# Multiplying the first two weight chunks behind six norms as a pair, contraction tile by contraction tile

## The reference, cut to what matters

```python
def _rmsnorm(x, w):
    xf = x.astype(jnp.float32)
    y = xf * lax.rsqrt(jnp.mean(xf * xf, axis=-1, keepdims=True) + EPS)
    return (y * w.astype(jnp.float32)).astype(x.dtype)
```

```python
def _conv_ffn(h, w_up, conv_w, w_down):
    u = _causal_dwconv(jnp.matmul(h, w_up), conv_w)
    gate, val = jnp.split(u, 2, axis=-1)
    return jnp.matmul(jax.nn.silu(gate) * val, w_down)
```

```python
        x = ffn_half_step(x, mx[0:3], g_ffn1[l], w_ffn1_gu[l], w_ffn1_down[l])
        hx = modulated_norm(x, g_mix[l], mx[3], mx[4])
        out_x = fourier_sgu_mixer(hx, ...)      # or attention in layer 1
        x = x + mx[5] * out_x
        x = ffn_half_step(x, mx[6:9], g_ffn2[l], w_ffn2_gu[l], w_ffn2_down[l])
```

## Time and profile before

| | before |
|---|---|
| median of 3 runs | 2116.26 us |
| the profiled execution | 2117.21 us |
| its span in the profile | 2115.1 us |
| TensorE busy (matmul) | 2043.2 us, 97% |
| VectorE busy | 1172.4 us, 55% |
| ScalarE busy | 821.3 us, 39% |
| mean granted TensorE clock | 0.992 |

### The profile page before, as it was taken

One profiled execution on the slowest core, in us unless ns is written; L12 is line 12 of the kernel. 1 busy time (PEld: TensorE's weight loads), 2 busy tenths in 40 slices (PEclk: granted clock), 3 DMA queues, 4 the chain that ended last, 5 costly groups with the idle time before them and its releaser, 6 DMA issues.

```text
span 2115.1 us, 30883 instructions
## 1 busy us (share of the span) xinstructions
PE 2043.2 (97%) x13253; PEld 1788.8 (85%) x13254; DVE 1172.4 (55%) x1579; ACT 821.3 (39%) x1049; POOL 224.8 (11%) x185
## 2 busy tenths in 40 slices
PE   6988999999999999999999999999999999999998
PEld 6985997999888888889888888888888888869998
DVE  6767555767653654453555442235766744655454
ACT  5642454655532222243342222234222223455444
POOL 1000000403111001100101001110100111001001
PEclk9999999999999999999999999999999999999999
DMA  6424654454642543352344332234545533304553
GB/s 240 158 84 179 221 199 180 148 182 162 227 161 93 189 146 135 107 187 89 120 159 153 122 136 88 82 127 168 196 162 201 189 116 113 125 20 160 172 182 114
DMA packets 54136, 317.05 MB, mean 150 GB/s; under 512 B 6000, under 2 KB 12400, under 8 KB 23792
## 3 DMA queue, kind: packets, MB, share of 16 engines
q1 hardware_dynamic: 50848, 308.99, 41.1%
q10 hardware_dynamic: 3152, 6.10, 0.8%
HBM read 314.01 MB, written 1.05 MB: 149 GB/s over the span
## 4 chain that ended last, share of the span: by engine, by line
PE 83%; DVE 8%; ACT 5%; issue 3%; DMA 1%; SPq 0%; DVEq 0%; ACTq 0%
PE psum L279 26%; PE psum L280 25%; PE psum L281 25%; ACT w_hi L255 3%; DVE w_lo L263 1%; PE psum L1316 1%; PE psum L1710 1%; DVE work L454 1%; DMA raw<-in_w_in_r 0%; DVE xc L1497 0%; PE psum L1330 0%; DVE small L1377 0%; DVE normed_lo L1890 0%; PE psum L918 0%; DVE work L1023 0%
## 5 line engine op out<-in xcount | busy, mean ns | idle before, releaser
L279 PE MATMUL psum<-normed_hi,w_hi 128*128 128x256 f32 (+1 forms) x2600 | 859.3, 330 | 20.0 <-DVE normed_lo L461 9.0
L280 PE MATMUL psum<-normed_lo,w_hi 128*128 128x256 f32 (+1 forms) x2600 | 848.8, 326 | 0.0
L281 PE MATMUL psum<-normed_hi,w_lo 128*128 128x256 f32 (+1 forms) x2600 | 848.5, 326 | 0.0
L263 DVE TENSOR_TENSOR w_lo<-raw,w_hi 128x2048 fp32r<-128x2048 f32 (+1 forms) x246 | 510.7, 2076 | 401.7 <-ACT w_hi L255 400.9
L279 PEld LDWEIGHTS psum<-normed_hi,w_hi 128*128 128x128 f32 x2600 | 492.9, 190 | 73.7 <-issue 23.6
L280 PEld LDWEIGHTS psum<-normed_lo,w_hi 128*128 128x128 f32 x2600 | 493.3, 190 | 43.0 <-issue 1.2
L281 PEld LDWEIGHTS psum<-normed_hi,w_lo 128*128 128x128 f32 x2600 | 492.9, 190 | 42.3
L255 ACT ACTIVATE w_hi<-raw 128x2048 fp32r<-128x2048 f32 (+1 forms) x246 | 421.7, 1714 | 167.4 <-PE psum L281 157.3
L279 PE MATMUL psum<-h_hi,w_hi 128*128 128x512 f32 (+1 forms) x913 | 310.6, 340 | 2.0 <-POOL h_lo L1655 1.7
L281 PE MATMUL psum<-h_hi,w_lo 128*128 128x512 f32 (+1 forms) x913 | 309.4, 339 | 0.0
L280 PE MATMUL psum<-h_lo,w_hi 128*128 128x512 f32 (+1 forms) x913 | 309.4, 339 | 0.0
(11 more groups left out here) (380 smaller groups left out, 1358.7 us busy)
## 6 DMA issues: line engine op xcount, KB each, us to landing
raw<-in_mod SPq DMA_DIRECT2D x72, 1024.0 KB, 4.7
raw<-in_a_up SPq DMA_DIRECT2D x42, 1024.0 KB, 4.8
raw<-in_b_up SPq DMA_DIRECT2D x42, 1024.0 KB, 4.8
raw<-in_ffn_up SPq DMA_DIRECT2D x22, 1024.0 KB, 4.9
raw<-in_a_down SPq DMA_DIRECT2D x32, 704.0 KB, 4.1
raw<-in_b_down SPq DMA_DIRECT2D x32, 704.0 KB, 4.1
raw<-in_ffn_down SPq DMA_DIRECT2D x16, 704.0 KB, 4.0
raw<-in_wo SPq DMA_DIRECT2D x8, 1024.0 KB, 4.8
```

What stands on the lines that cost most here:

```text
L263: dve.tensor_tensor(w_lo[:, slot, 0:size], raw[:, raw_slot(("main", g)), 0:size], w_hi[:, slot, 0:size].bitcast(F32), ALU.subtract).then_i ...
L279: pe.matmul(out, lh, rh, start=first, stop=False, skip_group_check=group)
L280: pe.matmul(out, lh, rl, start=False, stop=False, skip_group_check=group)
L281: return pe.matmul(out, ll, rh, start=False, stop=last, skip_group_check=group)
```

## The change

A method `pe_pair` takes the place of `pe_first` and of `ready_at_first` ahead of six jobs. `pe_feature_major` first waits for both of the first two chunks (their banks and their low parts), then hands both to `pe_pair`, and goes on with the third chunk as before. For the plain norms the first four contraction tiles are multiplied for both chunks (12 matmuls a tile), then tiles 4 to 7 of chunk 0, then tiles 4 to 7 of chunk 1. For a `HalfNorm` the first half of the columns is done for both chunks tile by tile, then the second half chunk by chunk; the sums of the second half move to the place behind tile 0. For the `FinalNorm` the order is context half of chunk 0, the 48 small matmuls, context half of chunk 1, sequence half of chunk 0, sequence half of chunk 1. `ready_at_first` and `pe_first` of `HalfNorm` stay for other jobs.

```diff
--- before.py
+++ after.py
@@ -280,10 +280,17 @@
             pe.matmul(out, lh, rl, start=False, stop=False, skip_group_check=group)
             return pe.matmul(out, ll, rh, start=False, stop=last, skip_group_check=group)
 
-        def pe_feature_major(pe, job, act_hi, act_lo, span, n_tiles=2, k_tiles=KT, before_k=None, after_chunk=None, k_order=None, in_halves=None):
+        def pe_feature_major(pe, job, act_hi, act_lo, span, n_tiles=2, k_tiles=KT, before_k=None, after_chunk=None, k_order=None, in_halves=None,
+                             first_pair=None):
 
             k_order = k_order or tuple(range(k_tiles))
-            for s in steps(job):
+            if first_pair is not None:
+                pair = steps(job)[:2]
+                for s in pair:
+                    bank_free(pe, s)
+                    pe.wait_ge(lo_ready, s.g + 1)
+                first_pair(pe, pair, act_hi, act_lo)
+            for s in steps(job)[0 if first_pair is None else 2:]:
                 bank_free(pe, s)
                 pe.wait_ge(lo_ready, s.g + 1)
                 if in_halves is not None and s.c in in_halves:
@@ -303,6 +310,14 @@
                 if after_chunk is not None:
                     after_chunk(s.c)
 
+        def pair_tile(pe, s, act_hi, act_lo, k, src, dst):
+
+            for n in range(2):
+                w = slice((n * KT + k) * P, (n * KT + k + 1) * P)
+                mm = three_passes(pe, psum[:, s.bank + n, dst], (w_hi[:, s.slot, w], w_lo[:, s.slot, w]),
+                                  (act_hi[:, k, src], act_lo[:, k, src]), k == 0, k == KT - 1)
+            return mm
+
         def pe_token_major(pe, job, act_hi, act_lo, span, after_tile=None):
 
             for s in steps(job):
@@ -476,6 +491,18 @@
             def ready(self, pe, k):
 
                 pe.wait_ge(n_lo, self.split_base + (k + 1) * self.halves)
+
+            def pe_pair(self, pe, pair, act_hi, act_lo):
+
+                for k in range(KT // 2):
+                    self.ready(pe, k)
+                    for s in pair:
+                        pair_tile(pe, s, act_hi, act_lo, k, self.span, slice(0, self.w))
+                for s in pair:
+                    for k in range(KT // 2, KT):
+                        self.ready(pe, k)
+                        mm = pair_tile(pe, s, act_hi, act_lo, k, self.span, slice(0, self.w))
+                    mm.then_inc(chunk_done, 1)
 
             def ready_at_first(self, pe):
 
@@ -1534,9 +1561,9 @@
                     if half:
                         pe_feature_major(pe, up, self.norm.hi, self.norm.lo, slice(0, self.w))
                     elif self.w > T:
-                        pe_feature_major(pe, up, xn_hi, xn_lo, slice(0, self.w), in_halves={0: self.norm.pe_first})
+                        pe_feature_major(pe, up, xn_hi, xn_lo, slice(0, self.w), first_pair=self.norm.pe_pair)
                     else:
-                        pe_feature_major(pe, up, self.norm.hi, self.norm.lo, slice(0, self.w), before_k=self.norm.ready_at_first(pe))
+                        pe_feature_major(pe, up, self.norm.hi, self.norm.lo, slice(0, self.w), first_pair=self.norm.pe_pair)
 
                     if half and late is not None:
                         late()
@@ -1822,6 +1849,22 @@
                                               (act_hi[:, k, t], act_lo[:, k, t]), k == 0, k == k_tiles - 1)
                 return mm
 
+            def pe_pair(self, pe, pair, act_hi, act_lo):
+
+                t = slice(0, T)
+                for k in range(KT):
+                    if k == 1:
+                        self.pe_sums(pe, 1)
+                    pe.wait_ge(n_lo, self.split_base + k + 1)
+                    for s in pair:
+                        pair_tile(pe, s, act_hi, act_lo, k, t, t)
+                t = slice(T, 2 * T)
+                for s in pair:
+                    for k in range(KT):
+                        pe.wait_ge(n_lo, self.split_base + KT + k + 1)
+                        mm = pair_tile(pe, s, act_hi, act_lo, k, t, t)
+                    mm.then_inc(chunk_done, 1)
+
             def act_square_half(self, act, h):
 
                 t, tile = slice(h * T, (h + 1) * T), slice(KT - self.tiles, KT)
@@ -1999,23 +2042,22 @@
                 dve.scalar_tensor_tensor(r, t, 1.5, r, ALU.add, ALU.mult).then_inc(n_rstd, 1)
                 dve.wait_ge(n_rstd, 2 * self.j + 2)
 
-            def pe_first(self, pe, s, act_hi, act_lo, n_tiles, k_tiles, k_order):
+            def pe_pair(self, pe, pair, act_hi, act_lo):
 
                 pe.wait_ge(n_lo, n20c.split_base + KT)
-                for h, t in ((1, C), (0, X)):
-                    for k in k_order:
-                        if h and k == 4:
+                for s in pair:
+                    for k in range(KT):
+                        if s.c == 0 and k == 4:
                             pe.wait_ge(final_sq, KT)
                             self.pe(pe)
-                        if not h:
-                            self.ready(pe, k)
-                        for n in range(n_tiles):
-                            w = slice((n * k_tiles + k) * P, (n * k_tiles + k + 1) * P)
-                            mm = three_passes(pe, psum[:, s.bank + n, t], (w_hi[:, s.slot, w], w_lo[:, s.slot, w]),
-                                              (act_hi[:, k, t], act_lo[:, k, t]), k == 0, k == k_tiles - 1)
-                    if h:
+                        pair_tile(pe, s, act_hi, act_lo, k, C, C)
+                    if s.c == 0:
                         mods_pe(pe, mods_behind("ffn_down1", 7))
-                return mm
+                for s in pair:
+                    for k in range(KT):
+                        self.ready(pe, k)
+                        mm = pair_tile(pe, s, act_hi, act_lo, k, X, X)
+                    mm.then_inc(chunk_done, 1)
 
             def dve_residual(self, dve):
 
@@ -2061,7 +2103,7 @@
             "gating_rsqrt", "gating_mixed", "branch_hi", "branch_lo"))
 
         def branch_pe(pe, norm, turn, closing):
-            pe_feature_major(pe, jobs["ab_a"], xn_hi, xn_lo, XC, in_halves={0: norm.pe_first})
+            pe_feature_major(pe, jobs["ab_a"], xn_hi, xn_lo, XC, first_pair=norm.pe_pair)
             turn()
             pe_token_major(pe, jobs["ab_v"], xn_hi, xn_lo, XC)
             pe_feature_major(pe, jobs["ab_u"], xn_hi, xn_lo, XC)
```

## The result

| | before | changed |
|---|---|---|
| median of 6 runs | 2117.46 us | 2124.99 us |
| range | 2115.16 to 2119.5 | 2123.3 to 2128.06 |
| the profiled execution | 2117.21 us | 2125.72 us |
| its span | 2115.1 us | 2123.9 us |

The ratio is 1.0038, with a 95% interval of 1.0027 to 1.0048. The forecast was 2124.7 us with a range of 2119.5 to 2128.0. In six runs of each, the difference of the medians is 7.5 us; the forecast was 8.4.

What follows compares the result with a forecast made beforehand. TensorE, busy for 97% of the span, was taken to set the time by its waits, columns and clock. Terms -3.3 + 5.7 + 2.9 + 0 + 1.9 + 1.2 = +8.4 us on 2116.3 gave 2124.7 us, range 2119.5 to 2128.

Steps and rivals of the forecast that it cites:

- The first step, the wait for chunk 1 at `n20`: At n20 the pair waits for chunk 1's low part before its first matmul, so TensorE starts 5.36 us late.
- The size of the term at `n20`: At n20, without the clock: 5.36 late start, -0.24 for the sums' wait, +0.61 for chunk 1's halves; +5.7 us.
- That the norm is hidden there: At n20 sums and norm come later, statistics at about 572.1 instead of 567.00, but the delay stays hidden.
- `ffn`, chunk 0 complete 24 matmuls late: At ffn chunk 0 ends after matmul 72, not 48, so chunk 2 starts late, once; +2.9 us, bounds 0 and 5.8.
- The halves: Behind n21, n22, n23: tile waits go, split width costs 0.61 us, two chunks take 24.0 us; -1.1 each, -3.3 us.
- The clock: Granted clock of 0.5 behind the new stalls: +1.9 us at n20, +1.2 at ffn, bounds 0 and 2.4 each.
- the nearest row: Profile row behind n25 used to price the low clock: 26 matmuls took 5.5 us instead of 3.12, 2.4 us lost.
- halving it at `ffn`: At ffn half the clock loss, +1.2 us, was taken because the stall is barely above the smallest that did it.
- `n25`: Behind n25: no wait but the first, half clock slower than VectorE's tiles, later splits have slack; 0, bounds -0.3 and +0.5.

Runs made afterwards that it cites:

- the kernel with part of the width given back: Pair kept only behind the three HalfNorms and n25, chunk 1's tiles 4 to 7 behind the HalfNorms at width 512; 2113.88 us, second run 2113.54 us.

## Why the prediction was right

- **The first step, the wait for chunk 1 at `n20`, is shown.** Forecast: TensorE starts 5.36 us late, released by `w_lo`. Measured: 5.04 us idle behind the last matmul's end, released by `w_lo` L263. Start to start it is 5.32 us (566.76 to 572.08) where it was 0.12 (561.53 to 561.65), so 5.20 us late against the job before. Moving the wait alone takes it away, undoing the pair takes it away.
- **The size of the term at `n20`**, forecast 5.7 us without the clock, is 5.3 (6.65 us for the stage, less 1.35). The error is in the path from the pair's start to the sequence half, which the sum took to be 0.24 us shorter than before and which is 0.7 us shorter.
- **That the norm is hidden there** held: VectorE's statistics start at 578.31, 11.6 us behind the start of the last matmul of the job before (566.76) instead of 5.5 (567.00 - 561.53), and still the sequence half never waits.
- **`ffn`, chunk 0 complete 24 matmuls late:** forecast 2.88 us, measured 2.89, once only. With half the tiles it is half.
- **The halves:** forecast 1.1 us a norm from 24.0 us for two chunks, measured 1.12 and 23.99. The 0.61 us for the split width, which decides that it is 1.1 and not 1.7, was measured by itself.
- **The clock** was the softest term. Forecast 1.9 us at `n20` and 1.2 at `ffn`, measured about 1.4 each time: at `n20` 1.35 from the filled stall; at `ffn` 1.5, from 4.4 us for the stage against 2.89 us of delay. The sum of the two was forecast at 3.1 and is 2.8. That the sum is closer than its terms is luck, since one was too high and the other too low. Why the nearest row was too dear is visible: of the eleven traces with an unfilled wait at `n25`, the slow stretch behind it covers over 5.5 us of matmuls in two (the kernel before and the run with the stall at `n20` filled) and 3.0 to 3.4 us in nine. So the 26 slow matmuls are the long case and 15 the short one. The reason given for halving it at `ffn`, that the stall is barely above the smallest that lowered the clock, has no support in the runs: the last section shows shorter ones that did.
- **`n25`:** forecast 0, with bounds of -0.3 and +0.5. The stage is 1.2 us shorter, outside the bounds, and all of it is the length of the slow stretch, not the pair; with the clock at 1.00 the pair takes 11.3 us, which is 96 matmuls of 256 columns.
- The terms add up to +6.7 + 4.4 - 3.4 = 7.7 us; the medians differ by 7.5. The other 1.1 us between the two profiled spans lie at the start (+0.6) and, with the clock, in the attention (+1.7) and behind `n25` (-1.2). The prediction had no term for these. They also moved in kernels that did not touch those places. That the forecast time of 2124.7 us lies 0.3 us from the measured one is luck too: the difference was forecast 0.9 us too large, and the median before came out 1.2 us above the one that the forecast started from.

## What to carry to other kernels

Widening a group of work so that it hides a paced producer also widens what must be ready before the group starts and delays what the group releases. So look for both ends of the group in the trace: the latest input of the second member, and the consumer that waits for the first member's completion. A wait belongs in front of the first instruction that needs it, not in front of the group: here moving the waits for one chunk was worth 6.2 us in the trace, more than the 4.3 us that the pair won at three norms in its best form. And a long idle stretch of TensorE had a second price behind it, 1.3 to 2.5 us here, which disposable matmuls, placed so that they did not delay the real ones, took away in two traces.

## What the runs showed of the hardware

- A dense stream of weight load and matmul in float32 halves runs 256 columns at 0.120 us behind `ffn` and the `HalfNorm`s and at 0.117 behind `n25`, and 512 at 0.227: half the columns cost 53% of the time. The activations behind `n25` are stored eight words further in their buffer than those behind `ffn`; that this makes the 3 ns was not tested, and the products of `h_hi` run at 0.117 too.
- The longer idle stretches were followed by a granted clock of 0.50 in every trace that has them: 5.0 to 5.3 us at `n20` in three, 3.7 us at `n25` in eleven, 2.9 us at `ffn` in four. The slow stretch cost 1.3 to 2.5 us. With 38 disposable matmuls in a stall of 5 us, of which 0.52 us stayed idle, the clock did not fall.
- Shorter ones give no line between falling and not falling. The 1.66 us ahead of `ffn` were followed by 1.00 in all twelve traces. But 2.34 us in the first block were followed by 0.50 in the kernel before (window 182.10) and by 1.00 in the run with the pair undone at `ffn`, and 1.54 us behind `n24` by 0.50, from 1.7 us after its end, in the run with the waits moved, where the kernel before has the same idle time and 1.00. The same idle time in the same code came out either way. In this order, the kernel before, the pair undone at `ffn`, the waits moved, the kernel before:

```profile
182.12 0.85 PE L1035 MATMUL psum<-work,head_rows 128*32 128x192 f32 x2 [2.34 <-DVE work L1023]
182.10:185.40 3.30, 3.27 (x11) 0.50 0.00 0
...
184.17 0.51 PE L1062 MATMUL psum<-work,head_rows 128*32 128x192 f32 x2 [2.34 <-DVE work L1050]
184.20:187.50 3.30, 3.25 (x18) 1.00 0.00 0
...
1790.11 0.36 PE L279 MATMUL psum<-normed_hi,w_hi 128*128 128x256 f32 x1 [1.54 <-DVE normed_lo L1933]
1791.80:1795.00 3.20, 3.20 (x13) 0.50 0.02 5
...
1790.02 0.35 PE L279 MATMUL psum<-normed_hi,w_hi 128*128 128x256 f32 x1 [1.54 <-DVE normed_lo L1890]
1791.80:1795.00 3.20, 3.20 (x26) 1.00 0.00 0
```

- In the attention of the last layer the granted clock was 1.00 from 1845 to 1860 us in one execution and 0.50 for 3.3 us or 6.6 us in others, in kernels with the same program there:

```profile
1840.20:1846.80 6.60, 6.60 (x32) 0.50 0.00 1
```

That is from the second run of the kernel with part of the width given back. It alone moves a single execution by about 1.5 to 3 us, as much as one term of this study. No experiment settled what decides it.
